# All eight samples' recurrence products in one run over four banks, and cached-value pairs at other ticks

## What is computed

```python
def gla_block(S, q, k, v, log_a):
    ...
    S_new = S * jnp.exp(b_last)[..., None] + jnp.einsum('bshk,bshv->bhkv', k_dec, v)
    return S_new, o_intra + o_inter

def diff_attn_sample(q, k_new, v_new, k_past, v_past, lam):
    ...
    p = jax.nn.softmax(s, axis=-1)
    a = (p[:, :, 0] - lam * p[:, :, 1]).astype(v_new.dtype)
    return (jnp.einsum('bhqk,bkhv->bqhv', a[..., :P], v_past)
            + jnp.einsum('bhqk,bkhv->bqhv', a[..., P:], v_new))
```

## Time and profile before

| | us |
|---|---|
| median of 3 runs | 1348.48 |
| lowest and highest | 1347.14, 1349.8 |
| the profiled execution | 1347.75 |
| its span | 1345.8 |
| TensorE busy, of the span | 1337.5 |
| VectorE busy | 890.9 |
| ScalarE busy | 577.6 |
| GpSimd busy | 394.7 |

### The profile page before, as it was taken

The page is one execution under the profiler, slowest core; times in us unless marked ns, Lnnn a source line. Parts: engine busy times, 40 slices in busy tenths (PEclk is TensorE's granted clock), DMA queues, the critical chain, the costliest instruction groups (busy, mean ns, idle before and its releaser), DMA issues.

```text
span 1345.8 us, 23939 instructions
## 1 busy us (share of the span) xinstructions
PE 1337.5 (99%) x8605; PEld 1122.0 (83%) x8605; DVE 890.9 (66%) x1619; ACT 577.6 (43%) x1078; POOL 394.7 (29%) x395
## 2 busy tenths in 40 slices
PE   9999999999999999999999999999999999999999
PEld 8778878777777777787777777667999999999998
DVE  6469667846758776767666674444566665887785
ACT  7463333425645563631424341232554354434532
POOL 3647425446515334351000000000432211332030
PEclk9999999999999999999999999999999999999999
DMA  9467744454366566686658565872565465133311
GB/s 326 128 192 215 243 134 142 141 161 138 95 198 195 174 214 179 211 244 231 224 200 280 186 234 172 303 263 89 197 208 186 171 219 173 48 110 110 111 33 64
DMA packets 126135, 240.33 MB, mean 179 GB/s; under 512 B 13673, under 2 KB 47258, under 8 KB 126018
## 3 DMA queue, kind: packets, MB, share of 16 engines
q1 hardware_dynamic: 116802, 214.68, 48.8%
q10 hardware_dynamic: 9216, 24.14, 5.2%
HBM read 198.16 MB, written 40.62 MB: 177 GB/s over the span
## 4 chain that ended last, share of the span: by engine, by line
PE 93%; DVE 3%; ACT 1%; issue 1%; DMA 1%; POOL 0%; SPq 0%; ACTq 0%; DVEq 0%; POOLq 0%
PE ps L87 26%; PE ps L89 25%; PE ps L88 25%; PE ps L1562 2%; PE ps L1381 2%; PE ps L3409 2%; PE ps L1599 2%; PE ps L1583 1%; PE ps L425 1%; PE ps L1797 1%; PE ps L1423 1%; DVE wl L832 1%; PE ps L487 1%; PE ps L488 1%; DMA out_v_prompt<-st 1%
## 5 line engine op out<-in xcount | busy, mean ns | idle before, releaser
L3168 POOL TENSOR_TENSOR kr<-kr,qb 128x512 f32<-128x512 f32 x128 | 174.1, 1369 | 160.7 <-DVE sd L3153 112.1
L87 PE MATMUL ps<-x2hB,uw_h 128*128 128x264 f32 (+1 forms) x512 | 145.1, 283 | 0.1
L88 PE MATMUL ps<-x2lB,uw_h 128*128 128x264 f32 (+1 forms) x512 | 144.7, 283 | 0.0
L89 PE MATMUL ps<-x2hB,uw_l 128*128 128x264 f32 (+1 forms) x512 | 144.5, 282 | 0.0
L87 PE MATMUL ps<-part_h,fh 128*128 128x264 f32 (+1 forms) x448 | 127.8, 285 | 0.0
L89 PE MATMUL ps<-part_h,fl 128*128 128x264 f32 (+1 forms) x448 | 127.0, 283 | 0.0
L88 PE MATMUL ps<-part_l,fh 128*128 128x264 f32 (+1 forms) x448 | 126.9, 283 | 0.0
L2934 DVE TENSOR_TENSOR xt<-xt,ps 128x264 f32<-128x264 f32 (+1 forms) x224 | 87.4, 423 | 35.7 <-PE ps L89 35.5
L3153 DVE TENSOR_REDUCE sd<-kr 128x8 f32<-128x512 f32 x128 | 85.3, 677 | 34.7 <-POOL kr L3168 34.7
L87 PE MATMUL ps<-x2hA,uw_h 128*128 128x512 f32 x256 | 105.0, 410 | 0.0
L87 PE MATMUL ps<-uh,dh 128*128 128x512 f32 x256 | 104.2, 407 | 0.4 <-DVE xt L2241 0.4
(11 more groups left out here) (392 smaller groups left out, 3403.3 us busy)
## 6 DMA issues: line engine op xcount, KB each, us to landing
kr<-in_cache_k SPq DMA_DIRECT2D x128, 256.0 KB, 3.1
raw_up<-in_w_up_units SPq DMA_DIRECT2D x64, 512.0 KB, 4.2
vr<-in_cache_v SPq DMA_DIRECT2D x128, 256.0 KB, 4.4
raw_dn<-in_w_down SPq DMA_DIRECT2D x32, 512.0 KB, 6.2
raw_dn<-in_w_down ACTq DMA_DIRECT2D x32, 512.0 KB, 4.7
raw<-in_w_in_units SPq DMA_DIRECT2D x23, 512.0 KB, 5.9
raw_up<-in_w_out_units SPq DMA_DIRECT2D x16, 512.0 KB, 4.1
kept_up_low<-uw_l SPq DMA_DIRECT2D x14, 512.0 KB, 6.5
```

What stands on the lines that cost most here:

```text
L87: pe.matmul(out, lh, rh, start=first and n == 0, stop=False, skip_group_check=onto)
L88: pe.matmul(out, lh, rl, start=False, stop=False, skip_group_check=onto)
L89: ins = pe.matmul(out, ll, rh, start=False, stop=last and n == len(ks) - 1, skip_group_check=onto)
L3168: pool.tensor_tensor(k[:, :], k[:, :], qb[v // PAGES][:, :], ALU.mult).then_inc(k_multiplied, 1)
```

## The change

Two things are changed.

In `sample_recurrence`, TensorE makes all 32 products in step 4, after all of `k_alone` is there, into banks 4 to 7, one bank for two samples; the waits on `st_updated` between them are gone. VectorE's four state updates come in steps 5, 6, 7 and 8. All other steps stay where they were.

In `program`, the ticks of `values` are no longer one after the other. Pairs come at the ticks of `pair_at`; the loads of the next pages and ScalarE's copy one tick later, and TensorE's reduction and VectorE's addition both in the tick ahead of the next pair.

```diff
@@ sample_recurrence, tensor
-        yield
-        yield
+        for _ in range(4):
+            yield
+        pe.wait_ge(k_alone_made, 13)
         for r in range(4):
-            pe.wait_ge(k_alone_made, 5 + 4 * (r // 2 + 1))
-            if r:
-                pe.wait_ge(st_updated, r)
             for x in (2 * r, 2 * r + 1):
                 for h in range(H):
-                    c = h % 2 * DH
-                    ins = pe.matmul(ps[c:c + DH, 5 + x % 2, h // 2 * DV:(h // 2 + 1) * DV], k_alone[x // 4][:, x % 4, h * DH:(h + 1) * DH],
+                    c, v0 = h % 2 * DH, x % 2 * 2 * DV + h // 2 * DV
+                    ins = pe.matmul(ps[c:c + DH, 4 + r, v0:v0 + DV], k_alone[x // 4][:, x % 4, h * DH:(h + 1) * DH],
                                     zs[:, 3, h * DV:(h + 1) * DV], start=True, stop=True, tile_position=(0, c))
             ins.then_inc(sg_pe, 1)
-            yield
+        for _ in range(6):
             yield
@@ sample_recurrence, vector
-        yield
-        yield
+        for _ in range(4):
+            yield
         for r_ in range(4):
             yield
...
-                    ins = dve.scalar_tensor_tensor(v, v, decay_s[:, 2 * x + t:2 * x + t + 1], ps[:, 5 + x % 2, t * DV:(t + 1) * DV],
+                    v0 = x % 2 * 2 * DV + t * DV
+                    ins = dve.scalar_tensor_tensor(v, v, decay_s[:, 2 * x + t:2 * x + t + 1], ps[:, 4 + r_, v0:v0 + DV],
                                                    ALU.mult, ALU.add)
             ins.then_inc(st_updated, 1)
+        for _ in range(3):
             yield
-        yield
@@ program
-        put("values", range(t1 + 12, t0 + FEED_TICKS))
+        pair_at = (79, 82, 85, 89, 92, 95, 98, 101, 104, 108, 111, 116, 121, 126, 131, 137)
+        put("values", [t1 + 12 + i for i in range(4)] + [t0 + pair_at[0] - 2])
+        for x, y in zip(pair_at, pair_at[1:]):
+            put("values", [t0 + x, t0 + x + 1, t0 + y - 1, t0 + y - 1])
+        put("values", range(t0 + pair_at[-1], t0 + FEED_TICKS))
```

## The result

| | before | after |
|---|---|---|
| median, us | 1348.27 (8 runs) | 1352.46 (8 runs) |
| lowest, highest | 1347.14, 1349.8 | 1351.73, 1354.39 |
| the profiled execution | 1347.75 | 1351.89 |
| its span | 1345.8 | 1350.2 |

The changed kernel is slower: the ratio of the times is 1.0029, with a 95% interval from 1.0020 to 1.0037, that is 2.7 to 5.0 us. The prediction was 1349.4 us, at most 1351.8; it was wrong.

The account below looks back on a forecast made before the run. TensorE, busy 1337.5 of 1345.8 us, was taken as the bound. Span 1345.8 - 0.58 + 0.07 + 1.2 + 0.2 = 1346.7; on the median 1348.48 + 0.9 = 1349.4 us, range 1346.9 to 1351.8.

Parts of the forecast that it names:

- The recurrence products: TensorE's four blocks of 8 products, 4.86 us in all: run together they enter and leave once, matmuls unchanged, 0.58 us less.
- The saved entries: Around TensorE's recurrence blocks: three fewer times entering and leaving the dense stream, 0.195 us each, 0.58 us less.
- The values' blocks: TensorE's value pairs and reductions: joining them to other side blocks saves 0.76 instead of 0.83 us, so costs 0.07 us.
- VectorE's stall: Down tile 6: TensorE waits for down tile 4's addition, late behind the moved state update; 1.2 us, bounds 0 and 1.6.
- The DMA queue: Page loads for value pairs at ticks 98 and 108, now closer to the pair before: typically no stall, 0.2 us taken.
- What else moves: VectorE's sums in the reduction's tick, at ticks 84 and 120, and ScalarE's copies: all nothing, up to 0.5 us.
- The rivals: Three other outcomes for the whole kernel: no stall at tick 60, pages come late, fewer breaks pay; chances 0.2, 0.17, 0.08.
- the stall came: Rival 1 claimed no stall at tick 60, VectorE being far enough ahead: 1348.0 us, chance 0.2.
- the pages were late: Rival 2 claimed slower page landings at the tighter value pairs: 1353.4 us, or 1350.8 in a milder case; chance 0.17.
- the breaks did not pay: Rival 3 claimed eight fewer breaks of the dense stream pay 0.2 us each, without any stall: 1346.9 us, chance 0.08.
- The chance of a slower kernel: For the whole kernel: slower 0.12, same 0.85, faster 0.03, with about 0.2%, 2.7 us, as what a measurement can tell.
- The prediction's own sign of being wrong: The kernel's span falling by over 1 us, or rising by over 3 through a load or chain held for hidden.

Follow-up runs that it names:

- late_update: The changed kernel with VectorE's fourth state update put back behind the softmax step: 1351.03 us, ratio 1.0014 to the kernel before.
- halves_cover: The kernel before with recurrence products in two runs of 16, in steps 4 and 2 swapped for none: steps 2 and 6, updates and pairs unmoved: 1348.65 us, ratio 0.9995.
- recur_only: The changed kernel with the value pairs at their old ticks, so the recurrence half alone: 1352.0 us, ratio 1.0026 to the kernel before.
- halves_early: The kernel before with recurrence products in two runs of 16, in steps 2 and 4, updates and value pairs unmoved: 1348.71 us, ratio 0.9998.
- two_runs: The changed kernel with the recurrence products in two runs of 16, 12 dense matmuls between them: 1350.86 us, ratio 1.0015 to the kernel before.
- small_run: The kernel before with its second block of 8 recurrence products made four times over, 32 in one run: 1353.85 us, ratio 1.0030.

## Why the prediction was wrong

- **The recurrence products.** This is the step that failed: "The matmuls themselves are the same." They are, but not the dense ones behind them. The clock was taken as 1.0 throughout, as it stood in the profile before, and no term or rival was given to what a run four times as long does to it. The clock fell to 0.51 behind the run and cost 1.56 us in the trace of the changed kernel. With it, the forecast would have been about 1351.0; the rest of the miss is in the terms below.
- **The saved entries** were predicted at 0.58 us and are 1.0. Blocks of 8, 16, 24 and 32 products cost 1.21, 2.085, 2.955 and 3.835 us: 0.875 for every 8 and 0.335 fixed. The prediction saw 0.09 on entering and 0.10 on leaving, and missed 0.14 between: the first dense matmul starts 620.71 - 619.69 = 1.02 us after the first product, not 0.875. The Trainium skill's page TensorE: Matmul & The Clock Gate (Single matmul latency), whose drain of about 175 ns gave an estimate of 1.05 us for six mode changes, was closer; this case's runs show 1.0, about 0.17 for each change. The prediction gave more weight to the earlier trace rows, but those are seams between two side blocks, and not the way out of the dense stream and back into it.
- **The values' blocks** were predicted at +0.07; their own cost did not move. The pair joined to the outputs costs 3.835 us, predicted 3.825, and joining it saves nothing. That a pair and the outputs are different tiling modes, so that the drain stays, is what TensorEngine Tiling (Array Packing), Key Properties in the Trainium skill led one to expect, and these rows agree.
- **VectorE's stall** was placed and caused as predicted (tile 6, the update ahead of the softmax, `late_update` shows it), and measured 1.33 us and 0.11 for the restart, against a predicted 1.2. A second stall, 0.36 us at tile 2, was missed. It is the same mechanism: the block that before stood at 619.69, just ahead of tile 2 at 620.71, gave VectorE's addition of tile 0, at 619.77 in the trace of before, its time. `halves_cover`, with a block in that place, has no wait there.
- **The DMA queue**: 0.2 us predicted, 0.22 measured in the one pair that had to wait, at tick 108, one of the two that were named. The pair at tick 98 did not wait.
- **What else moves** was taken at nothing, up to 0.5 us: it is 0.34 us at a third level and 0.25 at the first reduction. The third level's wait grew because a reduction that stood between two levels of that chunk had moved away, and so had 0.34 us of TensorE's time that covered VectorE's L1288. Such a loss of cover was sought at the down tiles only.
- **The rivals.** None of the three happened: the stall came, the pages were late by 0.2 us once, and the breaks did not pay. The chance of a slower kernel, 0.12, rested on the pages alone. The prediction's own sign of being wrong did come, a span up by over 3 us (1350.2 - 1345.8 = 4.4), but not for the reason given there, a load or a chain that was held for hidden: the largest part is the clock.

With the terms as measured: -1.0 + 1.56 + 0.36 + 1.44 in the recurrence's half, +0.8 in the values' half, 3.2 us. At their medians the changed kernel (+4.2) and `recur_only` (+3.2) were each about 1 us slower than their traces give (3.2 and 2.4, with the early start of before's profiled execution taken off), `late_update` (+2.2) was 0.7 us faster than its terms (-1.0 + 1.56 + 0.36 + 0.89 + 0.44 and 0.6 to 0.8 for the values, 2.9). The kernels that kept the clock lie nearer to theirs: `halves_early` -0.15 against +0.05, `halves_cover` -0.25 against -0.3, `two_runs` +2.05 against 2.3 to 2.5. All are inside the intervals. Executions also differ outside the changed stretch, by up to 1.9 us ahead of it and 2.1 behind it in these traces, which is more than what is missing. So the size of the clock's part is known from traces of single executions only: 1.55 to 1.56 us where the clock was low for 3.4 us, 3.1 in `small_run`, where it was low for 6.8. Its mean over executions was not settled.

## What to carry to other kernels

Before joining blocks of small matmuls, ask what the whole run does to TensorE's clock, not only what its seams save: read the granted clock in a window behind the longest run of tiles of the same shape, and if the new run is longer than any of that shape in the trace, give the drop a rival with a price, the dense steps that would run at half speed. The shape matters: the kernel before has a run of 32 other small products, whose clock of 1.00 would have misled here. The mean clock of a whole execution is too coarse for this; the timeline behind the run shows it. Breaks of a dense stream also cover other engines: for each block that is taken away, look at which wait ends just behind it, at every tile and not only at the one where work was added. A block's fixed cost is found by comparing blocks of different length, and not by looking at the steps at its two ends.

## What the runs showed of the hardware

- A TensorE that is never idle can still lose its clock. In all four traces with 32 products of 8 rows by 64 columns in one run it went from the granted 2.4 GHz level to 1.2: in three of them within 0.6 us behind a run of 3.6 us, and back 3.7 to 3.9 us after the run's end; in `small_run` already in the run, which so took 3.9, and back 6.1 us after its end. Behind 24 products (2.8 us) the traced execution lost it and four of eleven kept it; behind 16 (1.9 us) it was kept in four traces with two such runs each. The Trainium skill, TensorE: Matmul & The Clock Gate (Why this matters for your kernels), warns of idle gaps between bursts; here there was no gap. By the profile's busy times this was invisible: PE stood at 4.00 of 4.00 us.
- Fourteen matmuls of 128x128 in the same place, 3.2 us, and with the block 4.2, kept the clock at 1.00.
- Shape and not only size seems to matter. The kernel before has a run of the products of queries and states, tiles of 64 rows by 8 columns, as long as these, and the window behind it has a granted clock of 1.00. Which property of the two shapes makes the difference was not tried. The run and its window:

```profile
639.40 3.66 PE L3490 MATMUL ps<-st_new,q 64*8 64x128 f32 x64
```

```profile
640.00:648.00 8.00, 8.00 (x80) 6.46 (x75) 3.36 (x5) 0.63 (x1) 2.43 (x3) 1.00 0.26 103
```

- A block of these products costs about 0.335 us besides 0.109 for each product, and a wait of TensorE 0.11 us besides its own length, in the step behind it (0.34 instead of 0.2325).
